# Delta rule output summed in PSUM: queries scaled by the decay's exponential, one ScalarE step per chunk takes the sum out

## What is computed

```python
def gdn_chunk(S, inp):
    q, k, v, g, beta = inp
    gam = jnp.cumsum(g, axis=-1)
    ...
    u = U - jnp.einsum('bhtd,bhdv->bhtv', W, S)
    qk = jnp.einsum('bhtd,bhsd->bhts', q, k) * dec_incl
    o = jnp.einsum('bhtd,bhdv->bhtv', q * jnp.exp(gam)[..., None], S) + jnp.einsum('bhts,bhsv->bhtv', qk, u)
    g_last = gam[..., -1]
    S_new = jnp.exp(g_last)[..., None, None] * S + jnp.einsum(
        'bhsd,bhsv->bhdv', k * jnp.exp(g_last[..., None] - gam)[..., None], u)
    return S_new, o
```

## Time and profile before

| | |
|---|---|
| median of 3 runs | 698.5 us (698.24 to 699.27) |
| profiled execution, its own time | 698.49 us |
| its span, first to last instruction | 696.4 us |
| PE busy | 673.3 us, 97% |
| PE weight loads busy | 639.6 us, 92% |
| DVE busy | 413.0 us, 59% |
| POOL busy | 377.5 us, 54% |
| ACT busy | 319.5 us, 46% |
| mean granted clock of TensorE | 0.997 of full speed |

### The profile page before, as it was taken

One profiled execution on the slowest core, in us unless ns is written; L12 is line 12 of the kernel. 1 busy time (PEld: TensorE's weight loads), 2 busy tenths in 40 slices (PEclk: granted clock), 3 DMA queues, 4 the chain that ended last, 5 costly groups with the idle time before them and its releaser, 6 DMA issues. The chain is left out here.

```text
span 696.4 us, 13134 instructions
## 1 busy us (share of the span) xinstructions
PE 673.3 (97%) x4585; PEld 639.6 (92%) x4585; DVE 413.0 (59%) x984; ACT 319.5 (46%) x911; POOL 377.5 (54%) x581
## 2 busy tenths in 40 slices
PE   6899999999999999999999999999999999999995
PEld 4699999989999999989999999899999988888884
DVE  7736446278782372587833634888426267766257
ACT  6545441735644516456445254555452354342333
POOL 4446342368772343487924243888342558867323
PEclk9999999999999999999999999999999999999998
DMA  8745334222214347541649332203354315222014
GB/s 276 68 44 85 26 39 81 30 32 32 37 33 61 58 74 37 23 41 19 40 55 73 69 43 31 32 8 50 55 80 148 89 49 201 69 71 77 8 52 189
DMA packets 64005, 44.96 MB, mean 65 GB/s; under 512 B 17447, under 2 KB 59045, under 8 KB 63941
## 3 DMA queue, kind: packets, MB, share of 16 engines
q1 hardware_dynamic: 63908, 44.07, 37.0%
q10 hardware_dynamic: 32, 0.07, 0.0%
HBM read 35.88 MB, written 7.65 MB: 63 GB/s over the span
## 5 line engine op out<-in xcount | busy, mean ns | idle before, releaser
L279 PE MATMUL proj<-uTh,w_high 128*128 128x352 f32 (+4 forms) x768 | 262.0, 341 | 2.6 <-POOL w_low L567 2.6
L279 PE MATMUL proj<-uTh,w_low 128*128 128x352 f32 (+4 forms) x768 | 245.7, 320 | 0.0
L279 PE MATMUL proj<-uTl,w_high 128*128 128x352 f32 (+4 forms) x768 | 245.3, 319 | 0.0
L279 PEld LDWEIGHTS proj<-uTh,w_high 128*128 128x128 f32 x768 | 145.1, 189 | 2.9 <-issue 2.8
L279 PEld LDWEIGHTS proj<-uTl,w_high 128*128 128x128 f32 x768 | 145.1, 189 | 0.0
L279 PEld LDWEIGHTS proj<-uTh,w_low 128*128 128x128 f32 x768 | 144.3, 188 | 0.0
L324 POOL TENSOR_TENSOR w_low<-w_raw,w_high 128x256 fp32r<-128x256 f32 (+1 forms) x54 | 76.1, 1420 | 52.2 <-DVE decay L372 26.8
L1342 POOL TENSOR_TENSOR level_k<-hg_k,f_suffix 128x64 f32<-128x64 f32 (+1 forms) x144 | 66.6, 482 | 9.8 <-PE mix L1801 5.3
L1352 POOL TENSOR_TENSOR f_suffix<-f_suffix,f_prefix 128x192 f32<-128x192 f32 x84 | 51.8, 617 | 16.5 <-DVE f_prefix L1595 3.6
L1642 DVE SCALAR_TENSOR_TENSOR conv_out<-conv_in,hg_taps,conv_out 128x352 f32<-128x352 f32 (+2 forms) x81 | 54.1, 667 | 0.0
L1595 DVE TENSOR_TENSOR f_prefix<-f_prefix 128x192 f32<-128x192 f32 x84 | 42.5, 506 | 14.3 <-POOL f_suffix L1352 13.8
(11 more groups left out here) (328 smaller groups left out, 1410.8 us busy)
## 6 DMA issues: line engine op xcount, KB each, us to landing
w_raw<-in_w_in SPq DMA_DIRECT2D x32, 512.0 KB, 8.5
x_tile<-in_x SPq DMA_DIRECT2D x8, 512.0 KB, 8.7
w_raw<-y_scratch SPq DMA_DIRECT2D x8, 384.0 KB, 4.3
decay<-gamma_scratch SPq DMA_DIRECT2D x4, 576.0 KB, 3.9
landing<-in_w_out SPq DMA_DIRECT2D x4, 512.0 KB, 7.5
landing<-in_x SPq DMA_DIRECT2D x3, 512.0 KB, 5.8
out_y<-landing SPq DMA_DIRECT2D x3, 512.0 KB, 2.6
y_scratch<-gd_y SPq DMA_DIRECT2D x6, 192.0 KB, 1.8
```

The lines of the kernel that those rows point to most:

```text
L279: last = pe.matmul(acc[:, 0:tw], w[j % 2][:, k, :], u[:, k, t0:t0 + tw], start=(k == 0 and i == 0), stop=(k == KT - 1 and i == 2))
```

## The change

The queries take the factor exp(gam) themselves. The exponentials of `gamT` are formed once (ACT, tile `ageT`), stored in DRAM (`age_dram`), and each gd phase loads its head's nine rows over all partitions into the tile N, which is free until the block inverses are expanded into it. DVE multiplies xq by them after the scores, in front of `solve_blocks`. With that both parts of the output have the same factor, 1/|q|, so that q.S and QK.u can be summed in PSUM: TensorE puts q.S beside kd.u in the apply, in the second quarter of the bank that holds U, and adds QK.u to it. ACT takes the sum out, scaled by `rr[:, 1, c]`, one chunk later (in turn 0 of chunk c + 1), and the solve of chunk c + 1 waits for that. DVE's output step, its wait for ACT and the product of `cc` and `rr` go.

```diff
     gam_dram = nc.dram_tensor("gamma_scratch", [HEADS * NC, P], F32, kind="Internal").ap()
+    age_dram = nc.dram_tensor("age_scratch", [HEADS * NC, P], F32, kind="Internal").ap()
...
         load_decay(sp, 0, dec_in)
+        sp.wait_ge(age_set, 1)
+        sp.dma_start(age_dram, ageT[:, :]).then_inc(age_stored, 16)
         load_tile(5, tile_cols("hg", 1, 0))
         sp.wait_ge(raw_loaded[0], 48)
+        sp.wait_ge(age_stored, 16)
         leave(sp)
...
         take_gd_front(act, 4, split=False)
+        freed(act, front, "gam_rows")
+        act.activation(ageT[:, :], gamT[:, :], ACT.Exp).then_inc(age_set, 1)
         take_gd_front(act, 5, split=False)
...
     def pe_ask(pe, plan, c, state, kq_done):
-        rec, _ = take(pe, plan, ("rec", c))
+        rec = bank[plan.at[("rec", c)][0]]
         if c:
             pe.wait_ge(state, c)
-        last = pe.matmul(rec[:, 0:P], kT[:, chunk(c)], S_c[:, :], start=True, stop=True)
-        if c:
-            last = pe.matmul(rec[:, P:2 * P], xq[:, chunk(c)], S_c[:, :], start=True, stop=True)
-        last.then_inc(kq_done, 1)
+        pe.matmul(rec[:, 0:P], kT[:, chunk(c)], S_c[:, :], start=True, stop=True).then_inc(kq_done, 1)
-    def pe_solve(pe, plan, c, r_done):
+    def pe_solve(pe, plan, c, r_done, o_out):
         ap, done = take(pe, plan, ("U", c))
         pe.wait_ge(r_done, c + 1)
+        if c > 1:
+            pe.wait_ge(o_out, c - 1)
         pe.matmul(ap[:, 0:P], M[:, chunk(c)], r[:, :], start=True, stop=True).then_inc(done, 1)
-    def pe_apply(pe, plan, c):
+    def pe_apply(pe, plan, c, out_done):
...
         last = pe.matmul(bank[b][:, 2 * P:3 * P], kd[:, chunk(c)], u[:, :], start=True, stop=True)
         if c:
-            last = pe.matmul(bank[b][:, 3 * P:4 * P], QK[:, chunk(c)], u[:, :], start=True, stop=True)
+            o = bank[plan.at[("U", c)][0]]
+            last = pe.matmul(o[:, P:2 * P], xq[:, chunk(c)], S_c[:, :], start=True, stop=False)
         last.then_inc(mix_full[b], 1)
+        if c:
+            pe.matmul(o[:, P:2 * P], QK[:, chunk(c)], u[:, :], start=False, stop=True).then_inc(out_done, 1)
...
-    def act_out(act, plan, c, r_done, o_step):
+    def act_out(act, plan, c, out_done, o_out):
...
-        act.wait_ge(r_done, c + 1)
-        rec = bank[plan.at[("rec", c)][0]]
-        act.activation(osb[g % 2][:, chunk(i)], rec[:, P:2 * P], ACT.Copy, scale=cc[:, 1, c:c + 1]).then_inc(o_step, 1)
+        act.wait_ge(out_done, c)
+        o = bank[plan.at[("U", c)][0]]
+        act.activation(osb[g % 2][:, chunk(i)], o[:, P:2 * P], ACT.Copy, scale=rr[:, 1, c:c + 1]).then_inc(o_out, 1)
...
-    def dve_update(dve, plan, c, state, o_step):
+    def dve_update(dve, plan, c, state):
         rec = full(dve, plan, ("rec", c))
-        if c:
-            dve.wait_ge(o_step, c)
-        last = dve.scalar_tensor_tensor(out=S_c[:, :], in0=S_c[:, :], scalar=cc[:, 3, c:c + 1],
-                                        in1=rec[:, 2 * P:3 * P], op0=ALU.mult, op1=ALU.add).then_inc(state, 1)
-        if c == 0:
-            dve.wait_ge(state, 1)
-            dve.engine_nop().then_inc(bank_free(plan, ("rec", c)), 1)
-            return
-        g, i = divmod(c, GC)
-        dve.scalar_tensor_tensor(out=osb[g % 2][:, chunk(i)], in0=rec[:, 3 * P:4 * P],
-                                 scalar=rr[:, 1, c:c + 1], in1=osb[g % 2][:, chunk(i)],
-                                 op0=ALU.mult, op1=ALU.add).then_inc(bank_free(plan, ("rec", c)), 1)
+        dve.scalar_tensor_tensor(out=S_c[:, :], in0=S_c[:, :], scalar=cc[:, 3, c:c + 1],
+                                 in1=rec[:, 2 * P:3 * P], op0=ALU.mult, op1=ALU.add).then_inc(state, 1)
-    def act_squares(act, plan, g, ssq, before):
-        freed(act, plan, ("rec", GC * g + GC - 1))
+    def act_squares(act, plan, g, ssq, before, o_out):
+        act.wait_ge(o_out, GC * g + GC - 1)
...
             if GD_KINDS[j] == 0:
-                act.wait_ge(kq_done, (PAD + t0 + tw - 1) // P + 1)
+                act.wait_ge(out_done, (PAD + t0 + tw - 1) // P)
...
                 if c < NC:
-                    if turn == 0:
-                        act_out(act, plan, c, r_done, o_step)
-                    elif turn == 1:
+                    if turn == 1:
                         act_u(act, plan, c)
+                if turn == 0 and 0 < c <= NC:
+                    act_out(act, plan, c - 1, out_done, o_out)
...
             load_weights(sp, 2, tile_cols("hg", 3, h))
+            sp.dma_start(N[:, :], age_dram[h * NC:(h + 1) * NC, :].rearrange("(a c) t -> a (c t)", a=1).broadcast_to([P, NT])
+                         ).then_inc(age_in, 16)
...
                 scores(g)
+            dve.wait_ge(age_in, 16)
+            dve.tensor_tensor(xq[:, P:NT], xq[:, P:NT], N[:, P:NT], ALU.mult).then_inc(aged, 1)
             solve_blocks()
...
             for g in range(NG):
+                dve.wait_ge(aged, 1)
                 dve.wait_ge(n_in[g], 16 * GC)
...
-            dve.wait_ge(rq_done, 1)
-            dve.tensor_tensor(cc[:, 1, :], cc[:, 1, :], rr[:, 1, :], ALU.mult).then_inc(par, 1)
-            dve.wait_ge(par, 2)
             leave(dve)
```

More of the change, by code:

```diff
@@ L409, in hybrid_layer @@
     gamT = sb("gamma_rows", [HEADS * NC, P], F32, s1)
+    ageT = sb("age_rows", [HEADS * NC, P], F32, s1)
     ones = sb("ones", [P, P], F32, s1)
@@ L431, in hybrid_layer @@
     gam_stored, dec_in = sem("gam_stored"), sem("dec_in")
+    age_set, age_stored = sem("age_set"), sem("age_stored")
     tap0, conv_step, conv_done, silu = sem("tap0"), sem("conv_step"), sem("conv_done"), sem("conv_silu")
@@ L1152, in phase_hg @@
         halo, conv_step, conv_done, silu = sem("halo"), sem("conv_step"), sem("conv_done"), sem("conv_silu")
-        kq_done, r_done, state, o_step = sem("gd_kq"), sem("gd_rdone"), sem("gd_state_done"), sem("gd_o_step")
+        kq_done, r_done, state = sem("gd_kq"), sem("gd_rdone"), sem("gd_state_done")
+        out_done, o_out = sem("gd_out_done"), sem("gd_o_out")
         gd_ssq, gd_rstd, gd_eps, on_done = sem("gd_ssq"), sem("gd_rstd"), sem("gd_eps"), sem("gd_on")
@@ L1466, in past_act @@
                 if c < NC:
-                    if turn == 0:
-                        act_out(act, plan, c, r_done, o_step)
-                    elif turn == 1:
+                    if turn == 1:
                         act_u(act, plan, c)
+                if turn == 0 and 0 < c <= NC:
+                    act_out(act, plan, c - 1, out_done, o_out)
                 if v in SQUARES:
-                    act_squares(act, plan, SQUARES[v], gd_ssq, 0)
+                    act_squares(act, plan, SQUARES[v], gd_ssq, 0, o_out)
                 if v in NORMED:
@@ L1667, in past_dve @@
                     elif turn == 2:
-                        dve_update(dve, plan, c, state, o_step)
+                        dve_update(dve, plan, c, state)
                 if v in FINISHED:
@@ L1746, in past_pe @@
                     elif turn == 1:
-                        pe_solve(pe, plan, c, r_done)
+                        pe_solve(pe, plan, c, r_done, o_out)
                     else:
-                        pe_apply(pe, plan, c)
+                        pe_apply(pe, plan, c, out_done)
                 if v in TURNED:
@@ L1885, in phase_gd @@
         par = sem("gd_par")
-        rq_done = sem("rq_done")
+        age_in, aged = sem("age_in"), sem("gd_aged")
         ssq, rstd_s, kd_done = sem("gd_ssq"), sem("gd_rstd"), sem("gd_kd_done")
@@ L2012, in _ @@
             freed(pool, plan, ("qs", NG - 1))
-            rsqrt(pool, rr[:, 1, :], ss[:, 1, :], EPS * P, eps_added, NG + 1).then_inc(rq_done, 1)
+            rsqrt(pool, rr[:, 1, :], ss[:, 1, :], EPS * P, eps_added, NG + 1)
             for key in order:
```

## The result

The changed kernel takes 705.56 us (median; 705.24 to 706.26) where the kernel before takes 698.37 us (697.78 to 699.27). The ratio is 1.0087 with a 95% interval of 1.0067 to 1.0108: slower, by some 6 us (6.1 us of 698.5). The two medians are 7.2 us apart. The profiled execution took 705.32 us with a span of 703.6 us, against 696.4 before, so the profile shows 7.2 us as well. The change went in the direction that was forecast, by 1.6 to 1.9 times the +3.7 us. By the ratio it lies just inside the top of the range (+6.4 us), by the medians just over it.

A forecast was written before the change was run, and what follows sets the result against it. TensorE was taken as the bound. Relief -0.7, ScalarE wait +2.4 and gd product +2.0 summed to +3.7 us on the 696.4 us span, 700.1, or 702.2 us as measured time; range 697.4 to 704.9 us.

The forecast's parts named there:

- what bounds it: Whole kernel: TensorE, busy 673.3 of 696.4 us; work off VectorE or ScalarE pays only where TensorE waits for it.
- The relief: Hg phases: without VectorE's output step (L996) the ask at L935 waits less; 0.7 us gained, chunk 4 in three heads.
- the stop at chunk 6: Hg phases, heads 0 to 2: TensorE's solve waits 1.3 us for ScalarE's output of chunk 5, queued behind a SiLU.
- Not all of that stays: Chunk 6 stop: earlier waits at the apply absorb part; 0.8 us per head remains (bounds 0 and 1.3), 2.4 us for three.
- the gd term: Four gd phases: VectorE's new product delays the block solve; about 0.5 us each, 2.0 us in all (bounds 0 and 3.2).
- The row at 116.63: Gd phase before: a VectorE product took 1.75 us, 0.56 elsewhere, ending after GpSimd's split; read as the two taking turns.
- product first: Gd phase: VectorE's product runs ahead of GpSimd's power and split; the three need 0.6 us more than GpSimd alone.
- the middle value: Gd phase: 0.95 us taken as the block solve's delay, from cases of 0.6, 1.0 and 1.2 us.
- the cover: Gd phase, third expansion: TensorE needs it only at 122.10, so 0.53 us of delay is hidden, 0.43 after handover.
- the forecast sign, a wait at L2278: Gd phases: TensorE's loads waiting at L2278 for the third expansion would show the forecast right.
- the term 0: Gd phases: the extra 576 KB load lands in 3.9 us, long before VectorE needs it; cost 0.
- Rival (a): Only the ACT wait costs; in gd phases GpSimd's power doesn't hold the product; +1.7, 700.2 us, chance 0.17.

The follow-up runs named there:

- e8: The kernel before with VectorE's second output step (L996) left out of all 32 chunks, nothing else changed; ratio 0.9994 (0.9979 to 1.0010).
- e10: The changed kernel with ScalarE taking out only chunk 5's output in that chunk's own last turn, other outputs unmoved; ratio 0.9996 (0.9981 to 1.0010).
- the second execution: The changed kernel run and profiled again with no edit; ratio 1.0079 (1.0058 to 1.0100) to the kernel before.
- e4: The changed kernel with VectorE's product of queries and decay moved behind the block solve; ratio 1.0072 (1.0049 to 1.0095).
- e7: The changed kernel with VectorE's product cut from 1024 to 384 columns, load, place and waits kept; ratio 1.0051 (1.0027 to 1.0074).
- e1: The changed kernel without VectorE's product of the queries and the expansion's wait for it, the load kept; ratio 1.0069 (1.0042 to 1.0096).
- e2: The changed kernel without VectorE's product and without the load of the exponentials in the gd phases; ratio 1.0066 (1.0043 to 1.0088).
- e11: The changed kernel with chunk 5's output in that chunk's own last turn and VectorE's product behind the block solve; ratio 1.0002 (0.9989 to 1.0015).
- e3: The changed kernel with ScalarE taking every output out in turn 2 of its own chunk; ratio 1.0018 (0.9998 to 1.0039).

## Why the prediction was right or wrong

**Right: what bounds it, and that the busy time taken off VectorE is worth little.** The relief is 0.9 us by itself (e8), 0.7 forecast. The waits at the ask and at the apply went, as forecast.

**Right: the stop at chunk 6, its place, its cause and its size.** It is 1.47, 1.21 and 1.21 us, 1.3 forecast; none in head 3. Its phase is 0.2 us longer in every version of the change. There PE's loads have one wait that was not there before, 0.33 us at a level product 16.0 us behind the phase's start; what brings it was not followed further.

**Wrong: "Not all of that stays", 0.8 us a head.** This term was +2.4 us; e10 shows 5.1 us (4.6 against the second execution). The prediction let PE's waits at the apply of chunks 6 and 7, 0.44 and 0.58 us in the order of before (head 0; 0.17 and 0.58 in the others), pay for part of the stop. They did not pay: in e10, which has the changed order without the stop, PE's loads wait at the apply in one place, for 0.2 us. (Waits under 0.15 us are in no view.) The prediction did see ScalarE fall behind through the transposes and let the apply of chunk 7 move by 0.7 us. In hg 1 it stands 0.9 us later than before, and 1.35 us later than in e10, and the whole stop is still there at chunk 8's ask. With the whole stop carried, the upper bound that stood in the prediction, the term would have been 3.9 us; 4.0 is measured with GpSimd's form the same on both sides. The other 1.1 us were in no term. They go with turns between GpSimd and VectorE that come out otherwise in most hg phases of the changed kernel.

**Half right: the gd term, 2.0 us.** Its mechanism holds: a longer split, a later block solve, gone when the product moves (e4) or is short (e7). Its size is 0.5 us for three phases. The row at 116.63 on which it rests was read rightly: the split beside it, not among the rows shown, runs from 115.57 to 117.97 us, and VectorE's product ends at 118.38. Two steps failed. GpSimd's power did not hold the product, which started 0.45 us before the power's end. So "product first" was the case to take, with a forecast delay of 0.6 us (0.52 measured) and not the middle value of 0.95. And the cover is large against it: 0.13 to 0.19 us are left per phase, so that it took 0.34, and 0.43 was forecast, which is close. In gd 0 to 2 the third expansion is awaited only in the first execution, where block moves are late too; so the forecast sign, a wait at L2278, took them as well. The Trainium skill (SBUF — State Buffer, section Who interferes with whom) has a VectorE instruction with two SBUF inputs and a GpSimd instruction that reads SBUF exclude each other for a whole instruction. By this trace that holds for the split beside the product (2.39 to 3.05 us), not for the power on nine columns, although GpSimd's spans are rough. The copy behind it (0.17 to 0.70 us) has one input and ends when the split has; the same section counts copies among the steps that can take the shared port.

**Missing: block moves that take longer in some executions.** They put 2.1 us on the profiled execution of the changed kernel in gd 0 to 2, and so brought the gd phases (3.0 us for 2.0) near the forecast by luck. A forecast of 0.5 a phase looked confirmed by gd 1 (+0.61) and gd 2 (+0.54) until the second execution.

**The load and the front.** The load lands in 10.5 us, not in 3.9: it goes behind the weights' load. Nobody waited for it, so the term 0 stands (e1 against e2: 1.0069 and 1.0066).

**The sum, mended,** without the front: for the first execution -0.5 (the relief as far as it arrives in e10) + 4.0 (stop) + 1.1 (GpSimd's form) + 0.5 (product) + 0.2 (hg 3) + 2.1 (block moves) + 0.4 (gd 3) = +7.8 us; for the second -0.5 + 4.0 + 0.6 + 0.5 + 0.2 + 0.7 (gd 3) = +5.5 us. These terms are differences between the profiled phases, so that they must add up; they explain no more than the comparisons behind them. The two ratios, 1.0079 and 1.0087, are 5.5 and 6.1 us. The forecast of +3.7 had the stop 1.6 us too small, had nothing for the turns (0.6 to 1.1 us), for hg 3 and for gd 3, and had the product 1.5 us too large. That it came as near as it did is in part luck. Rival (a), only the ACT wait, was the nearer one in mechanism; its price had the same faulty term. Its time, 700.2 us, is farther off than the forecast's. The test "wrong as a whole if the waits at L1800 and L1801 move by more than 1 us" was a bad one: L1802 has 4.5 us for 3.0, but e10 has 4.4 there and loses nothing. The waits moved; the sum of all waits of PE's loads in the hg phases is about the same in e10 as before (12.6 and 12.7 us).

## What to carry to other kernels

When a new wait stops an engine whose order is fixed, follow the instructions queued behind it to their readers, until they come back to the engine that stopped. Idle time counted in the old order may not be there in the new one: look whether it is, before it pays for anything. A step of 0.35 us that moves from a free engine to one that also feeds others costs by its place in that engine's order: here three of 32 outputs, chunk 5's in three heads, queued behind a SiLU, cost 4 us. The place of the others shows no price of its own: e3 and e10 differ by 0.8 us, and that is GpSimd's form. And take a second profile of the changed kernel before sizing a term under 1 us a phase.

## What the runs showed of the hardware

A GpSimd step on nine columns that lasts 2.14 us (101.52 to 103.66) didn't hold back a VectorE product of two SBUF tiles: the product ran from 103.21 to 104.43 us and took 1.22 us, as long as alone at 113.29 in e4. A GpSimd split of [128x1024] got 0.66 us longer by 0.8 us of overlap with the same product. Where two products of SBUF tiles on the two engines met in the hg phases, the one that started first kept its length, by a lead of 0.03 us in e11; the other grew by 0.17 us (VectorE's) or 0.33 us (GpSimd's). The block moves on SP's queue, six of them, took 3.8 to 3.9 us in 47 of the 52 gd phases of all profiles and 4.3 to 4.7 us in five (4.49 in the first execution of the changed kernel, 4.66 in gd 3 of the kernel before), with nothing in the profile's rows that names the cause.
